# A two-block transformer on one core: GpSimd adds the shift rows behind w_out, VectorE squares the first feed-forward's relu

## The chip, the core and the metric

The kernel runs on one core of a Trainium2 chip. A core has TensorE (PE, the matrix engine), VectorE (DVE), ScalarE (ACT), GpSimd (POOL) and SyncE (SP, which here only issues DMAs); each engine works through its own queue in order and waits on semaphores. The metric is device time in microseconds (us), as the median of several runs. Lower is better.

## What is computed

Two transformer blocks on a sequence of 1024 rows of 1024 float32 values. What matters here of the first is its feed-forward, and of the second its output projection and the norm that follows:

```python
# first block, last step
h = h + jnp.square(jax.nn.relu(_rms_norm(h, norm_ff_g[l]) @ ff_w1[l])) @ ff_w2[l]
return _rms_norm(h, final_norm_g)
...
# second block
mod = c_act @ w_ada[l] + b_ada[l]
sh1, sc1, ga1, sh2, sc2, ga2 = [m[:, None, :] for m in jnp.split(mod, 6, axis=-1)]
...
x = x + ga1 * (mixed @ w_out[l])
h2 = rmsnorm(x, g_ffn[l]) * (1.0 + sc2) + sh2
gate, up = jnp.split(h2 @ w_gu[l], 2, axis=-1)
x = x + ga2 * ((jax.nn.silu(gate) * up) @ w_down[l])
```

The feed-forward is 1024 to 4096 to 1024 in the first block. `sh2` is one row of 1024 values that is added to every row.

## The kernel before, in words

The kernel is written as a row of phases. In each, every engine has its own program (`@block.tensor`, `@block.vector` and so on), all engines meet at the phase's end, and the order of the instructions on an engine is the order in which the program writes them. A float32 product is computed as three float32r matmuls on high and low halves (`mm3`, L187 to L189), so each left and right operand exists as a rounded high part (written by ScalarE) and a low part (VectorE: value minus high part). PSUM has 8 banks of 128 x 512 float32.

**The first feed-forward** (`phase_ffn` with `gated=None`, L2417) runs over 16 groups `g` of 256 hidden features. A group has an up half of four units `u = 4g + 2f + half` (two blocks `f` of 128 features, two halves of 512 rows) into banks 0 to 3, and a down half of 16 tiles (two column halves of 8 row tiles) into banks 4 to 7. TensorE runs up(g) and then down(g-1). For each unit ScalarE takes the relu out of PSUM into `first[half]` (L2556), GpSimd squares it into `full[half]` (L2600), ScalarE rounds it to the high part (`ft.hi`, L2543), and VectorE makes the low part (L2626). VectorE also adds the 16 down tiles to `h` (L2634, `sums`), makes the low parts of the next weights (L2620, L2667), and in the first 12 groups does eight multiply-adds for the second block's modulation, two behind each unit (`ModulationSum.add`, L2220 and L2223). TensorE writes down tile t+4 into the bank of tile t, so it waits for VectorE's sum of tile t. Signals: `bank_free` is raised by the relu, `square_done` by the square, `ft_hi` and `ft_lo` by the two parts.

VectorE's program in a group is: for each of the four units m, the low part of unit m-1, then two multiply-adds; behind the fourth also the low part of a down weight; then two sums, the low part of the fourth unit, two sums, a weight, and so on.

**The second block's output projection** (`phase_rows_gemm_norm` with `modulated`, L1810) multiplies by w_out in four sweeps p of eight row tiles t: column half c = p // 2, inner half p % 2. A row tile is 12 matmuls of 128x512. In the last sweep the norm runs beside the matmuls (`StreamNorm`, L281). Row t goes through: VectorE adds PSUM to the residual (L1933, `add`), ScalarE squares and sums (L308), takes a root (L350), VectorE inverts it (L355) and scales the row by it and the gain (L360) into one of two buffers `tmp[t % 2]`, TensorE turns the row (`turn`: 8 blocks of 128x128) into two banks, ScalarE writes the high part (L387, `high`), and VectorE the low part (L392, `low`). TensorE does turn(t-2) behind the matmuls of tile t. The shift `sh2` enters in the turn: the banks are begun with two matmuls of the shift row's high and low part (L371, L372, on 8 partitions), and then the row's blocks are multiplied by the identity and accumulated (L378) instead of transposed (L376). `ShiftRows` (L410) makes the two parts; they are loaded with a 4 KB DMA.

The orders that decide what waits for what in the last sweep:

```python
# VectorE, t = 0 .. 9
add(1, t); norm.scale(dve, t - 1); norm.low(dve, t - 2)
# ScalarE, t = 0 .. 9
norm.high(act, t - 2); norm.square(act, TT + t); norm.root(act, t)
```

The same phase runs twice in the first block without modulation: there `turn` is 8 transposes (L376) and nothing is added. GpSimd in this phase only scales two weight pieces by the gate (L1908).

Of the kernel before, what the change touches and what calls it, by code (L numbers as in the profile page):

```python
# [14 lines left out]
P = 128  # L15
# [105 lines left out]
class Core:  # L121


    def __init__(self, nc, ap):
# [10 lines left out]
            "bank_free", "ft_hi", "ft_lo", "table0", "table1", "table2", "table3", "mirrored", "selected", "row_ready_dve", "probs_turned", "mod_ready", "bias_zero", "ada_bias0", "ada_bias1", "mod_loaded", "mod_gain_loaded", "mod_summed", "mod_out", "mod_gain_ready", "mod_stored", "x_stored", "gate_loaded", "half_squared", "half_gained", "half_second", "row_base", "row_first", "row_bias", "shift_loaded", "shift_hi", "shift_lo", "row_squared", "row_root", "row_inverse", "row_scaled", "row_turned", "row_hi", "row_lo", "gain_loaded", "x0", "x1", "x2", "x3", "x4", "x5", "x6", "x7", "ada0", "ada1", "ada2", "ada3", "ada_summed", "ada_spilled", "w2_scaled", "mirror_copied",  # L135
# [145 lines left out]
class StreamNorm:  # L281
# [5 lines left out]
    def __init__(self, core, h, dst, gain, tmp_kb, junk_kb, ready, pairs=None, first_gain=None, shift=None):  # L287
        self.core, self.h, self.dst, self.gain, self.ready, self.pairs = core, h, dst, gain, ready, pairs
        self.first_gain, self.shift = first_gain, shift
# [72 lines left out]

    def turn(self, pe, t):
        nc, S = self.core.nc, self.core.sig
        pe.wait_ge(S["row_scaled"].sem, S["row_scaled"].at(t + 1))
# [28 lines left out]
    def close(self):  # L394
# [5 lines left out]
        if self.dst is not None:  # L400
            for n in ("row_turned", "row_hi", "row_lo"):
                S[n].close(TT)
        if self.first_gain is not None:
# [1406 lines left out]
def phase_rows_gemm_norm(core, lhs, w, h, dst, gain_name, gain_kb, tmp_kb, junk_kb, residual, ring_kb=(102, 118, 134), ahead=0, following=(), modulated=None):  # L1810
# [11 lines left out]
    summed = lambda n: S["dve_free"].at(n + 1)  # L1822
    shift, carried = None, core.tiny2[:, 256:264]
    if modulated is not None:
        gate, next_gate, shift = core.view(modulated[0], D), core.view(modulated[1], D), ShiftRows(core, modulated[2], 3 * D)
    norm = StreamNorm(core, h, dst, gain, tmp_kb, junk_kb, (S["dve_free"], summed), BEHIND, shift=shift and shift.operands())
    plain_gain = gain if modulated is None else norm.tmp[:, 0, :]
    with nc.Block() as block:
        @block.sync
        def _(sp):  # L1830
            for p in range(4):
# [6 lines left out]
                if p == R - 1:  # L1838
# [12 lines left out]
        def _(pe):  # L1851
            def turn(t):
# [5 lines left out]
                if t == 0 and modulated is not None:  # L1858
                    pe.wait_ge(S["shift_lo"].sem, S["shift_lo"].at(1))
                norm.turn(pe, t)  # L1860

            for p in range(4):
                c, kh = p // 2, p % 2
                pe.wait_ge(S["w_lo"].sem, S["w_lo"].at(p + 1))
                for t in range(TT):
# [8 lines left out]
                    if p == 3 and t >= 2:  # L1874
                        turn(t - 2)
# [1384 lines left out]
```

## Time and profile before

| | us |
|---|---|
| median of 3 runs | 4066.36 (4063.68 to 4066.87) |
| the profiled execution, its device time | 4063.24 |
| its span, first to last instruction | 4061.4 |
| TensorE busy | 3631.5 (89%) |
| VectorE busy | 1998.9 (49%) |
| ScalarE busy | 1121.2 (28%) |
| GpSimd busy | 541.7 (13%) |
| mean granted TensorE clock, 1 is full speed | 0.937 |

The first feed-forward fills about 1617 to 2340 us of the span, the last sweep of the second block's output projection with its norm 3259 to 3311 us. The percentages are averages over phases with different limits; what a change is worth has to be read in its own phase.

### The profile page before, as it was taken

The numbers are of one execution on the slowest core, as the hardware profiler recorded it, in microseconds if no ns is written. First come the engines' busy times: TensorE is split into PE (matmuls) and PEld (weight loads), VectorE is DVE, ScalarE is ACT, GpSimd is POOL, SyncE is SP. The second block draws the span as 40 slices with busy tenths as digits, with TensorE's granted clock in tenths as the row PEclk, the third lists the DMA queues.
The fourth block names the chain that finished last, engine by engine and source line by source line (L and its number), as shares of the span: only waits on it lengthen the run. The fifth ranks groups of instructions, "written<-read, shape, count | busy, mean of one in ns | idle before, by whom it ended". The sixth has DMA issues, their size and how long they took to land. (4 is left out here: it accounts for less than half of the span.)

```text
span 4061.4 us, 43012 instructions
## 1 busy us (share of the span) xinstructions
PE 3631.5 (89%) x16474; PEld 2856.8 (70%) x16474; DVE 1998.9 (49%) x3148; ACT 1121.2 (28%) x2006; POOL 541.7 (13%) x377
## 2 busy tenths in 40 slices
PE   7868696896978879999999998889989899999998
PEld 6736475773667757788888775766668777888886
DVE  3264645314744143555553438789975433333243
ACT  3233232323333132211211324124445321111112
POOL 0046564000010000101100100000034201000000
PEclk8969798897989999999999999999999999999999
DMA  2012123100022111323221211100000211111111
GB/s 94 27 33 74 42 79 106 31 32 4 1 91 83 57 47 34 97 93 121 93 93 60 84 52 37 47 20 22 11 14 1 99 37 52 52 49 49 47 52 52
DMA packets 210515, 220.07 MB, mean 54 GB/s; under 512 B 15523, under 2 KB 148548, under 8 KB 210098
## 3 DMA queue, kind: packets, MB, share of 16 engines
q1 hardware_dynamic: 210356, 217.90, 16.9%
q8 instruction: 106, 1.74, 0.2%
q14 instruction: 53, 0.43, 0.0%
HBM read 205.79 MB, written 11.55 MB: 54 GB/s over the span
## 5 line engine op out<-in xcount | busy, mean ns | idle before, releaser
L187 PE MATMUL psum<-rounded,rounded 128*128 128x512 f32 (+2 forms) x3936 | 1544.7, 392 | 216.5 <-POOL rounded L906 86.0
L188 PE MATMUL psum<-rounded,rounded 128*128 128x512 f32 (+2 forms) x3936 | 1536.2, 390 | 0.0
L189 PE MATMUL psum<-rounded,rounded 128*128 128x512 f32 (+2 forms) x3936 | 1534.1, 390 | 0.0
L187 PEld LDWEIGHTS psum<-rounded,rounded 128*128 128x128 f32 x3936 | 752.0, 191 | 384.0 <-POOL rounded L906 90.8
L189 PEld LDWEIGHTS psum<-rounded,rounded 128*128 128x128 f32 x3936 | 751.4, 191 | 153.1
L188 PEld LDWEIGHTS psum<-rounded,rounded 128*128 128x128 f32 x3936 | 751.9, 191 | 150.2 <-issue 0.2
L2634 DVE TENSOR_TENSOR plain<-psum,plain 128x512 f32<-128x512 f32 x432 | 288.5, 688 | 112.0 <-PE psum L189 110.6
L2645 DVE TENSOR_TENSOR plain<-psum,plain 128x512 f32<-128x512 f32 x44 | 30.4, 692 | 437.3 <-ACT plain L2554 437.3
L3052 POOL TENSOR_TENSOR plain<-plain,plain 128x128 f32<-128x128 f32 (+3 forms) x64 | 89.4, 1408 | 717.4 <-ACT plain L3123 695.4
L2626 DVE TENSOR_TENSOR rounded<-plain,rounded 128x512 fp32r<-128x512 f32 x108 | 97.2, 900 | 174.8 <-ACT rounded L2543 174.7
L2915 DVE MAX8 plain<-plain 128x8 f32<-128x384 f32 (+5 forms) x192 | 170.6, 889 | 4.0
L2917 DVE MATCH_REPLACE8 plain<-plain,plain 128x384 f32<-128x384 f32 (+5 forms) x192 | 168.1, 876 | 0.0
L2554 ACT ACTIVATE plain<-psum 128x512 f32<-128x512 f32 x44 | 26.3, 599 | 470.3 <-PE psum L189 470.3
L2612 POOL TENSOR_TENSOR plain<-plain,plain 128x1024 f32<-128x1024 f32 x22 | 53.4, 2429 | 748.2 <-DMA plain<-in_w_down_dram 748.2
L2990 PE MATMUL psum<-plain,plain 64*128 64x512 f32 (+7 forms) x384 | 151.2, 502 | 0.0
L906 POOL TENSOR_TENSOR rounded<-plain,rounded 128x512 fp32r<-128x512 f32 x96 | 133.3, 1402 | 128.9 <-ACT rounded L901 128.7
L2600 POOL TENSOR_TENSOR plain<-plain 128x512 f32<-128x512 f32 x64 | 67.2, 1050 | 606.2 <-ACT plain L2556 606.2
L2556 ACT ACTIVATE plain<-psum 128x512 f32<-128x512 f32 x64 | 38.3, 598 | 380.3 <-PE psum L189 380.3
L2576 ACT ACTIVATE rounded<-plain 128x1024 fp32r<-128x1024 f32 x54 | 57.1, 1057 | 278.6 <-DMA plain<-in_ff_w_dram 160.6
L3071 DVE CUSTOM_DVE_ANT_0 plain<-psum,plain 128x128 f32<-128x128 f32 (+7 forms) x128 | 96.4, 753 | 69.1 <-PE psum L2990 38.1
L3125 ACT ACTIVATE plain<-plain,plain 128x128 f32<-128x128 f32 (+7 forms) x128 | 98.8, 772 | 56.7 <-DVE plain L3074 56.0
L901 ACT ACTIVATE rounded<-plain 128x512 fp32r<-128x512 f32 x96 | 58.7, 629 | 178.3 <-DMA plain<-in_c_fwd_dram 103.5
(284 smaller groups left out, 3935.8 us busy)
## 6 DMA issues: line engine op xcount, KB each, us to landing
plain<-in_ff_w_dram SPq DMA_DIRECT2D x64, 512.0 KB, 5.5
plain<-in_w_ada_dram SPq DMA_DIRECT2D x96, 256.0 KB, 3.1
plain<-in_w_gu_dram SPq DMA_DIRECT2D x44, 512.0 KB, 4.9
plain<-in_w_in_dram SPq DMA_DIRECT2D x36, 512.0 KB, 3.7
plain<-in_c_fwd_dram SPq DMA_DIRECT2D x64, 256.0 KB, 2.6
plain<-in_w_down_dram SPq DMA_DIRECT2D x22, 512.0 KB, 3.2
plain<-in_c_inv_dram SPq DMA_DIRECT2D x32, 256.0 KB, 2.6
plain<-in_x_dram SPq DMA_DIRECT2D x2, 4096.0 KB, 15.5
```

Source lines behind the costliest of these rows:

```text
L187: nc.tensor.matmul(out, wh, xh, start=first, stop=False)
L188: nc.tensor.matmul(out, wh, xl, start=False, stop=False)
L189: return nc.tensor.matmul(out, wl, xh, start=False, stop=last)
L906: self.core.nc.gpsimd.tensor_tensor(w.lo, w.raw, w.hi_raw, ALU.subtract).then_inc(S["ft_lo"].sem, 1)
L2626: nc.vector.tensor_tensor(ft[b].lo[:, f, cols], full[half], ft[b].hi_raw[:, f, cols], ALU.subtract).then_inc(S["ft_lo"].sem, 1)
L2634: nc.vector.tensor_tensor(hv, ps[:, 4 + t % 4, :], hv, ALU.add).then_inc(S["dve_free"].sem, 1)
L2915: nc.vector.max(best, sc).then_inc(self.done, 1)
L2917: nc.vector.match_replace(out=sc, in_to_replace=best, in_values=sc, imm_value=TAKEN).then_inc(self.done, 1)
L2990: last = nc.tensor.matmul(ps[:, 2 * (n % 2) + a // BANK, 0:b - a], q, k[:, a:b], start=True, stop=True)
L3052: nc.gpsimd.tensor_tensor(tb[n % 2][:, 0:w], biases[h % 2][:, L - w:L], sel_tile(core, i), ALU.add).then_inc(S["pool_done"].sem, 1)
L3071: nc.vector.tensor_tensor_reduce(out=sc[n % 2][:, 0:w], in0=pair(n, w), in1=b, scale=SCALE, scalar=-3.0e38, op0=ALU.add, op1=ALU.max, accu ...
L3125: nc.scalar.activation(sc[n % 2][:, 0:w], sc[n % 2][:, 0:w], ACT.Exp, bias=stat[:, n % 16, 1:2], accum_out=stat[:, n % 16, 2:3]).then_inc( ...
```

## The change

It has two parts that share nothing.

In the first feed-forward, GpSimd no longer squares. VectorE multiplies the unit's PSUM bank by its relu (`first[half]`), which gives the same square. It does this at the head of each unit in its program, before the low part of the unit before. TensorE's bank is now free when the square is done.

Behind w_out the shift is a full tile of 1024 columns, the same row on all 128 partitions. It is loaded by a 512 KB DMA into the place of the first gate, once the fourth weight piece is scaled. GpSimd adds it to each scaled row in `tmp`; TensorE waits for this (`row_added`) and turns the row with 8 transposes. TensorE does turn(t-3) behind tile t, not turn(t-2), so that turn(4) comes behind tile 7 and turns 5, 6 and 7 follow it. `ShiftRows` is no longer used here.

```diff
@@ StreamNorm
+    def add(self, pool, t, row):
+        nc, S, tmp = self.core.nc, self.core.sig, self.tmp[:, t % 2, :]
+        pool.wait_ge(S["row_scaled"].sem, S["row_scaled"].at(t + 1))
+        nc.gpsimd.tensor_tensor(tmp, tmp, row, ALU.add).then_inc(S["row_added"].sem, 1)
+
     def turn(self, pe, t):
-        pe.wait_ge(S["row_scaled"].sem, S["row_scaled"].at(t + 1))
+        if self.added:
+            pe.wait_ge(S["row_added"].sem, S["row_added"].at(t + 1))
+        else:
+            pe.wait_ge(S["row_scaled"].sem, S["row_scaled"].at(t + 1))
@@ phase_rows_gemm_norm
+    late = 2 if modulated is None else 3
-        gate, next_gate, shift = core.view(modulated[0], D), core.view(modulated[1], D), ShiftRows(core, modulated[2], 3 * D)
-    norm = StreamNorm(core, h, dst, gain, tmp_kb, junk_kb, (S["dve_free"], summed), BEHIND, shift=shift and shift.operands())
+        gate, next_gate, shift = core.view(modulated[0], D), core.view(modulated[1], D), core.view(modulated[0], D)
+    norm = StreamNorm(core, h, dst, gain, tmp_kb, junk_kb, (S["dve_free"], summed), BEHIND, added=modulated is not None)
@@ its SyncE
-                        shift.load(sp)
+            if modulated is not None:
+                sp.wait_ge(S["w2_scaled"].sem, S["w2_scaled"].at(4))
+                sp.dma_start(shift, core.modulations[:, 3 * D:4 * D].partition_broadcast(P)).then_inc(S["shift_loaded"].sem, 16)
@@ its TensorE
-                if t == 0 and modulated is not None:
-                    pe.wait_ge(S["shift_lo"].sem, S["shift_lo"].at(1))
-                    if p == 3 and t >= 2:
-                        turn(t - 2)
-            turn(6)
-            turn(7)
+                    if p == 3 and t >= late:
+                        turn(t - late)
+            for t in range(TT - late, TT):
+                turn(t)
@@ its ScalarE, VectorE
-                shift.high(act)
-                    shift.low(dve)
@@ its GpSimd
+                pool.wait_ge(S["shift_loaded"].sem, S["shift_loaded"].at(16))
+                for t in range(TT):
+                    norm.add(pool, t, shift)
@@ phase_ffn, TensorE (gated is None)
-                            pe.wait_ge(S["bank_free"].sem, S["bank_free"].at(u - 3))
+                            pe.wait_ge(S["square_done"].sem, S["square_done"].at(u - 3))
@@ phase_ffn, GpSimd
-                            nc.gpsimd.tensor_tensor(full[half], first[half], first[half], ALU.mult).then_inc(S["square_done"].sem, 1)
-                over_groups(pool, squares)
@@ phase_ffn, VectorE
-                    if gated is not None:
-                        dve.wait_ge(S["act_done"].sem, S["act_done"].at(u + 1))
-                        if not (known(u) and u < 2):
-                            dve.wait_ge(S["ft_lo"].sem, S["ft_lo"].at(u - 1))
-                        nc.vector.tensor_tensor(full[half], ps[:, 2 * half + 1, :], first[half], ALU.mult).then_inc(S["square_done"].sem, 1)
+                    dve.wait_ge(S["act_done"].sem, S["act_done"].at(u + 1))
+                    if not (known(u) and u < 2):
+                        dve.wait_ge(S["ft_lo"].sem, S["ft_lo"].at(u - 1))
+                    bank = 2 * half + 1 if gated is not None else 2 * f + half
+                    nc.vector.tensor_tensor(full[half], ps[:, bank, :], first[half], ALU.mult).then_inc(S["square_done"].sem, 1)
```

VectorE in the first feed-forward's loop, from the low part of the third unit (before) or the square of the fourth (after) to the first sum of the group. L numbers of the changed kernel are some lines higher: L2626 is L2629, L2223 is L2235, L2667 is L2670, L2634 is L2637. Before:

```order
L2626 TENSOR_TENSOR rounded_2048_7326<-plain_512_1401,rounded_2048_7325 128x512 [waits ft_hi]
L2222 REGISTER_ALU [waits ada2]
L2223 SCALAR_TENSOR_TENSOR plain_512_10320<-plain_512_1409,plain_64_52,plain_512_10320 128x512 [waits ada_summed]
L2222 REGISTER_ALU [waits ada3]
L2223 SCALAR_TENSOR_TENSOR plain_512_10320<-plain_512_1408,plain_64_52,plain_512_10320 128x512 [waits ada_summed]
L2666 ISA
L2667 TENSOR_TENSOR rounded_1024_67<-plain_1024_70,rounded_1024_64 128x1024 [waits v_hi]
L2632 REGISTER_ALU
L2634 TENSOR_TENSOR plain_8192_4835<-psum,plain_8192_4835 128x512 [waits aux_done]
```

And in the changed kernel:

```order
L2648 TENSOR_TENSOR plain_512_1400<-psum,plain_512_1396 128x512 [waits ft_lo,act_done]
L2627 REGISTER_ALU
L2629 TENSOR_TENSOR rounded_2048_7326<-plain_512_1401,rounded_2048_7325 128x512 [waits ft_hi]
L2234 REGISTER_ALU [waits ada2]
L2235 SCALAR_TENSOR_TENSOR plain_512_10320<-plain_512_1409,plain_64_52,plain_512_10320 128x512 [waits ada_summed]
L2234 REGISTER_ALU [waits ada3]
L2235 SCALAR_TENSOR_TENSOR plain_512_10320<-plain_512_1408,plain_64_52,plain_512_10320 128x512 [waits ada_summed]
L2669 ISA
L2670 TENSOR_TENSOR rounded_1024_67<-plain_1024_70,rounded_1024_64 128x1024 [waits v_hi]
L2635 REGISTER_ALU
L2637 TENSOR_TENSOR plain_8192_4835<-psum,plain_8192_4835 128x512 [waits aux_done]
```

One instruction more, the square, stands ahead of an order that is otherwise the same.

TensorE in the last sweep of the second block's output projection, one turn and the matmuls behind it (`plain_896_49` holds the identity, `plain_2048_9062` the two row buffers, `rounded_8_...` the shift's parts). Before:

```order
L371 MATMUL psum<-rounded_8_21830,rounded_128_21828 128x512 [waits row_scaled,dve_free]
L372 MATMUL psum<-rounded_8_21830,rounded_128_21829 128x512
L378 MATMUL psum<-plain_896_49,plain_2048_9062 128x128 x4
L371 MATMUL psum<-rounded_8_21830,rounded_128_21828 128x512
L372 MATMUL psum<-rounded_8_21830,rounded_128_21829 128x512
L378 MATMUL psum<-plain_896_49,plain_2048_9062 128x128 x4
L187 MATMUL psum<-rounded_2048_9617,rounded_8192_21649 128x512
```

And in the changed kernel:

```order
L187 MATMUL psum<-rounded_2048_9617,rounded_8192_21622 128x512
L188 MATMUL psum<-rounded_2048_9618,rounded_8192_21622 128x512
L189 MATMUL psum<-rounded_2048_9617,rounded_8192_21623 128x512
L384 MATMUL psum<-plain_896_49,plain_2048_9062 128x128 [waits row_added,dve_free]
L384 MATMUL psum<-plain_896_49,plain_2048_9062 128x128 x7
L187 MATMUL psum<-rounded_2048_9617,rounded_8192_21622 128x512
```

The four matmuls of the shift are gone, the eight products with the identity are transposes (L384 is L376 of before), and the wait is on GpSimd's addition. GpSimd's queue in that phase, from the two scaled weight pieces on, before:

```order
L1908 TENSOR_TENSOR plain_2048_9057<-plain_2048_9057,plain_1024_19025 128x2048 [waits loaded2]
L1908 TENSOR_TENSOR plain_2048_9619<-plain_2048_9619,plain_1024_19025 128x2048 [waits loaded0]
L1828 UNCONDITIONAL_BRANCH
L2605 UNCONDITIONAL_BRANCH [waits barrier_Pool_Activation_PE_DVE_SP_gather]
L2612 TENSOR_TENSOR plain_1024_66<-plain_1024_66,plain_1024_21826 128x1024 [waits loaded]
```

And in the changed kernel:

```order
L1918 TENSOR_TENSOR plain_2048_9057<-plain_2048_9057,plain_1024_18998 128x2048 [waits loaded2]
L1918 TENSOR_TENSOR plain_2048_9619<-plain_2048_9619,plain_1024_18998 128x2048 [waits loaded0]
L366 TENSOR_TENSOR plain_2048_9062<-plain_2048_9062,plain_1024_18998 128x1024 [waits row_scaled,shift_loaded]
L366 TENSOR_TENSOR plain_2048_9062<-plain_2048_9062,plain_1024_18998 128x1024 [waits row_scaled] x7
L1839 UNCONDITIONAL_BRANCH
```

Eight additions of 128x1024 come behind the weight pieces, each waiting for VectorE's scaled row.

## Rows read from the trace of the kernel before

**Rows 1.** Waits, 1620 to 2345 us: engine, line, waited for: us in total, times, longest.

```profile
PE psum L187 <- DVE rounded L2620: 5.6, 1, 5.6
PE psum L187 <- DVE plain L2634: 2.0, 11, 0.2
```

**Rows 2.** Timeline, one group: start, us, engine, line, operation, shapes, count, [idle before].

```profile
1760.47 0.60 ACT L2556 ACTIVATE plain<-psum 128x512 f32<-128x512 f32 x1 [3.37 <-PE psum L189]
1761.22 1.04 POOL L2600 TENSOR_TENSOR plain<-plain 128x512 f32<-128x512 f32 x1 [4.40 <-ACT plain L2556]
1761.62 1.19 DVE L2626 TENSOR_TENSOR rounded<-plain,rounded 128x512 fp32r<-128x512 f32 x1 [2.79 <-ACT rounded L2543]
1764.18 1.22 DVE L2667 TENSOR_TENSOR rounded<-plain,rounded 128x1024 fp32r<-128x1024 f32 x1
1765.31 1.28 DVE L2634 TENSOR_TENSOR plain<-psum,plain 128x512 f32<-128x512 f32 x2
1765.48 0.39 PE L189 MATMUL psum<-rounded,rounded 128*128 128x512 f32 x1
1766.05 0.50 PE L187 MATMUL psum<-rounded,rounded 128*128 128x512 f32 x1 [0.18 <-DVE plain L2634]
1766.51 0.68 DVE L2626 TENSOR_TENSOR rounded<-plain,rounded 128x512 fp32r<-128x512 f32 x1
```

**Rows 3.** Stretches: length, PE, PEld, DVE, ACT, POOL busy, PEclk, DMA, GB/s.

```profile
3262.00:3308.00 46.00, 45.51 (x237) 33.87 (x236) 25.29 (x31) 14.64 (x31) 0.00 (x0) 1.00 0.14 37
1252.00:1262.00 10.00, 2.79 (x23) 2.13 (x20) 6.72 (x8) 5.55 (x10) 0.00 (x0) 0.93 0.06 16
20.00:25.00 5.00, 3.06 (x16) 2.43 (x16) 4.91 (x7) 3.42 (x8) 0.00 (x0) 0.66 0.76 184
```

**Rows 4.** Timeline, TensorE: two turns with the shift, two of the first block's w_out without.

```profile
3276.59 0.48 PE L187 MATMUL psum<-rounded,rounded 128*128 128x512 f32 x1
3282.77 0.48 PE L187 MATMUL psum<-rounded,rounded 128*128 128x512 f32 x1
...
1240.75 1.03 PE L376 MATMUL psum<-plain,plain 128*128 128x128 f32 x8
1244.36 1.04 PE L376 MATMUL psum<-plain,plain 128*128 128x128 f32 x8
1254.12 1.06 PE L376 MATMUL psum<-plain,plain 128*128 128x128 f32 x8 [1.46 <-DVE plain L360]
```

**Rows 5.** Timeline, VectorE, the last sweep: two additions, a scaled row, the last low part.

```profile
3261.88 0.75 DVE L1933 SCALAR_TENSOR_TENSOR plain<-plain,plain,psum 128x512 f32<-128x512 f32 x1 [22.84 <-PE psum L189]
3264.53 0.75 DVE L1933 SCALAR_TENSOR_TENSOR plain<-plain,plain,psum 128x512 f32<-128x512 f32 x1 [1.90 <-PE psum L189]
3265.39 1.28 DVE L360 SCALAR_TENSOR_TENSOR plain<-plain,plain,plain 128x1024 f32<-128x1024 f32 x1
3310.07 1.23 DVE L392 TENSOR_TENSOR rounded<-psum,rounded 128x1024 fp32r<-128x1024 f32 x1 [2.74 <-ACT rounded L387]
```

**Rows 6.** Groups by line and shape; one line's durations (min/median/max ns).

```profile
L387 ACT ACTIVATE rounded<-psum 128x1024 fp32r<-128x1024 f32 x32 | 32.8, 1025 | 64.5 <-PE psum L378 39.9 <-PE psum L376 24.5
L3052 POOL TENSOR_TENSOR plain<-plain,plain 128x1024 f32<-128x1024 f32 x8 | 18.9, 2357 | 3.4 <-DVE plain L3071 3.4
L1074 POOL TENSOR_TENSOR plain<-plain,plain x16: 1292/1742/1762, 346.6 to 614.5; 128x512 f32<-128x512 f32 x16
```

**Rows 7.** Timeline, VectorE beside a GpSimd instruction that reads SBUF.

```profile
3188.97 8.85 DVE L1916 TENSOR_TENSOR rounded<-plain,rounded 128x2048 fp32r<-128x2048 f32 x2 [3.22 <-ACT rounded L1889]
3190.66 5.01 POOL L1908 TENSOR_TENSOR plain<-plain,plain 128x2048 f32<-128x2048 f32 x1 [5.43 <-DMA plain<-in_w_out_dram]
3227.60 4.47 DVE L1916 TENSOR_TENSOR rounded<-plain,rounded 128x2048 fp32r<-128x2048 f32 x2
...
2322.05 10.76 POOL L314 TENSOR_TENSOR plain<-plain,plain 128x512 f32<-128x512 f32 x8 [33.31 <-ACT plain L308]
2323.17 0.69 DVE L2634 TENSOR_TENSOR plain<-psum,plain 128x512 f32<-128x512 f32 x1 [0.67 <-PE psum L189]
```

More of the change, by code:

```diff
@@ L281, with __init__ @@
 class StreamNorm:
-    def __init__(self, core, h, dst, gain, tmp_kb, junk_kb, ready, pairs=None, first_gain=None, shift=None):
+    def __init__(self, core, h, dst, gain, tmp_kb, junk_kb, ready, pairs=None, first_gain=None, shift=None, added=False):
         self.core, self.h, self.dst, self.gain, self.ready, self.pairs = core, h, dst, gain, ready, pairs
-        self.first_gain, self.shift = first_gain, shift
+        self.first_gain, self.shift, self.added = first_gain, shift, added
         self.tmp = core.view3(tmp_kb, 2, D)
@@ L402, in close @@
                 S[n].close(TT)
+        if self.added:
+            S["row_added"].close(TT)
         if self.first_gain is not None:
@@ L1889, in _ @@
                 nc.scalar.activation(ring[p % R].hi, ring[p % R].raw, ACT.Copy).then_inc(S["w_hi"].sem, 1)
-            if modulated is not None:
-                shift.high(act)
             for n in range(TT):
@@ L1961, in phase_rows_gemm_norm @@
     if modulated is not None:
-        shift.close()
+        S["shift_loaded"].close(16)
         S["w2_scaled"].close(4)
@@ L2525, in _ @@
             if modulation is not None:
-                pe.wait_ge(S["bank_free"].sem, S["bank_free"].at(4 * G))
+                pe.wait_ge(S["square_done"].sem, S["square_done"].at(4 * G))
                 tail.total(pe)
@@ L2555, in group @@
                         else:
-                            nc.scalar.activation(first[half], ps[:, 2 * f + half, :], ACT.Relu).then_inc(S["bank_free"].sem, 1)
+                            nc.scalar.activation(first[half], ps[:, 2 * f + half, :], ACT.Relu).then_inc(S["act_done"].sem, 1)
                         if (f, half) != (0, 0):
@@ L2592, in _ @@
             def _(pool):
-                def squares(g, b, n):
-                    for f in range(2):
-                        for half in range(2):
-                            u = unit(g, f, half)
-                            pool.wait_ge(S["bank_free"].sem, S["bank_free"].at(u + 1))
-                            if not (known(u) and u < 2):
-                                pool.wait_ge(S["ft_lo"].sem, S["ft_lo"].at(u - 1))
-                            nc.gpsimd.tensor_tensor(full[half], first[half], first[half], ALU.mult).then_inc(S["square_done"].sem, 1)
                 modulation.clear(pool)
-                over_groups(pool, squares)
                 tail.multiply(pool)
@@ L2639, in group @@
                     u = unit(g, f, half)
-                    if gated is not None:
-                        dve.wait_ge(S["act_done"].sem, S["act_done"].at(u + 1))
-                        if not (known(u) and u < 2):
-                            dve.wait_ge(S["ft_lo"].sem, S["ft_lo"].at(u - 1))
-                        nc.vector.tensor_tensor(full[half], ps[:, 2 * half + 1, :], first[half], ALU.mult).then_inc(S["square_done"].sem, 1)
+                    dve.wait_ge(S["act_done"].sem, S["act_done"].at(u + 1))
[3 more added lines that the diff above has]
+                    nc.vector.tensor_tensor(full[half], ps[:, bank, :], first[half], ALU.mult).then_inc(S["square_done"].sem, 1)
                     if m:
@@ L2684, in phase_ffn @@
         S[n].close(k * G)
-    if gated is None:
-        S["bank_free"].close(4 * G)
-    else:
-        S["act_done"].close(4 * G)
+    S["act_done"].close(4 * G)
+    if gated is not None:
         S["w2_scaled"].close(2 * G)
```

4 lines of the change are left out of this document (2 added, 2 removed).

## The prediction

> **What bounds the kernel now.** TensorE is busy 89% of the span, so a gain has to come from a pause or from work of TensorE itself. I read the two stages that the change touches, first by the waits, then by the timeline. "No change" is within 0.2%, 8.1 us, about what a measurement of this kernel can tell.
>
> In the first feed-forward TensorE hardly pauses: one wait of 5.6 us for VectorE's weight part (L2620) in the first group, and 11 short ones for a sum (L2634) [rows 1]. One of the 11 is drawn out [rows 2]: a matmul takes 0.23 us of TensorE (additions 2.65 to 2.7 us apart for tiles of 12 [rows 5]), but the one behind 1765.48 starts at 1766.05, so it is 0.34 late. It waits for the first sum of the group (1765.31), which VectorE began late. Looking back: ScalarE's relu ends at 1761.07, GpSimd squares 1761.22 to 1762.26, and VectorE's low part, begun at 1761.62, takes 1.19 us. The same instruction takes 0.68 at 1766.51, with no GpSimd work beside it.
>
> In the last sweep of the second block's output projection TensorE is the bound: 45.5 of 46 us busy at full clock [rows 3]. One tile with its turn takes 6.18 us (3276.59 to 3282.77); the same phase in the first block takes 3.61 (1240.75 to 1244.36) with plain transposes [rows 4]. So 2.57 us per row is the price of the shift on TensorE. From the first addition to the end of the last low part the sweep takes 3261.88 to 3311.30, 49.4 us [rows 5].
>
> **What GpSimd's port does.** Two low parts of 128x2048 take 4.47 us when GpSimd rests, and 8.85 when GpSimd scales a weight (5.01 us) meanwhile [rows 7]: the 4.4 us more say that VectorE stood still for most of GpSimd's instruction. But a sum out of PSUM takes 0.69 us in the middle of GpSimd's work [rows 7], no more than alone. I take from this: VectorE with two SBUF operands and GpSimd exclude each other; VectorE with one operand in PSUM is free. The Trainium skill says the same (SBUF — State Buffer, "Who interferes with whom"): the loser blocks for the whole instruction. By that rule the feed-forward's part of the change is helped and the sweep's part is hurt, since VectorE's scaled row reads h and the gain from SBUF.
>
> **Part 1, the square on VectorE.** GpSimd's 64 squares go. VectorE gets 64 instructions out of PSUM of the kind of L2634, 0.61 to 0.69 us each (two in 1.28), and three low parts of four lose the 0.51 us of blocking [rows 2]. At the critical place: relu ends 1761.07; square 1761.11 to 1761.72; low part 0.6, to 1762.3; the two multiply-adds with the low part of the down weight up to the first sum keep their distance of 2.6 us behind the low part (1761.62 + 1.19, less 0.08 by which neighbours overlap, is 1762.73; the sum starts at 1765.31); so the first sum starts at 1764.9 to 1765.0, not 1765.31. TensorE's 0.34 us of lateness is just covered: 11 x 0.34 = 3.8 us less. In the first group the same 0.3 us is taken from the one long wait, whose weight part stands behind the fourth unit. Sum 4.1 us less. The modulation's rows, for which VectorE waits early in a group, are asked for at TensorE's pace; the squares stand ahead of that wait only where their relu is done before the rows land, so I cost this at nothing. TensorE's wait for `square_done` of four units earlier looks back a whole group: nothing. Bounds: 0 (the pause stays, because something else is late) and 5.
>
> **Part 2, the addition on GpSimd.** Removed: the shift's four matmuls per row and the slower products; a 4 KB DMA and three tiny instructions ahead of the sweep, where TensorE does not wait for them. Added: a 512 KB DMA on SyncE's queue behind the fourth scaled weight, 30 us before it is needed and ahead of nothing that is due; and 8 GpSimd instructions of 128x1024. L3052 does such an addition in 2.36 us; L1074, the dearest per element, needs 1.74 for half the size, 3.5 for this [rows 6]. I take 2.36, since both its operands are plain rows as here.
>
> TensorE alone would go at 3.61 a row. The new bound is the chain of a row, because two row buffers and the orders on VectorE and ScalarE close a loop over two rows: low(t-2) stands ahead of add(t+1), and scale(t) needs it. From one scaled row to the next but one: scale 1.28, hand-over to GpSimd 0.15 (as relu to square in rows 2), addition 2.36, hand-over 0.1, turn 1.0 (1.06 when it stands alone [rows 4]), high part 1.03 [rows 6], hand-overs 0.15, low part 1.15 (1.23 less the overlap), and 0.9 from an addition's start to its scaled row (3264.53 to 3265.39 [rows 5]): 8.1 us for two rows, 4.05 each. The port alone would give scale 1.28, addition 2.36 and hand-overs, some 3.9: nearly the same.
>
> The sweep then, counted from the first addition: first scaled row done at 4.8 [rows 5], added at 7.3; TensorE's fourth tile ends at 3 x 2.7 = 8.1 (the pace of the additions in rows 5); turn(0), high, low until 11.3; add and scale of row 2 until 13.5; GpSimd until 16.0; turn(2) at 16.1. Five rows of 4.05 bring turn(7) to 36.35, and turn, high and low part end it at 39.6. Against 49.4 this is 9.8 less.
>
> The clock: behind tile 7, TensorE only turns four rows in some 13 us. In the first block, 28% busy with turns, it kept full clock for most of 1252 to 1262 us (mean 0.93) [rows 3]: it fell near 1260.6, 8.8 us behind the last matmul. So I expect the last turn at half speed, about 0.9 us more. Between 0 and two turns, 1.8.
>
> **Sum.** -4.1 - 9.8 + 0.9 = -13.0 us. Against the profiled execution's own 4063.24 us this is 4050.2. That execution is 3.1 us below the median of the runs shown, 4066.36; the same difference gives 4053.4 us.
>
> **The rivals.** (a) GpSimd's addition is dear: 3.5 us, or it also stops VectorE's instructions out of PSUM. The first makes a row 1.28 + 3.5 + 0.3 = 5.1 us or a little less in total, and the sweep 47; the second puts low part and addition behind GpSimd too, about 6 a row, and the sweep 49.5. For it: GpSimd instructions of up to 1.74 for 512 columns exist. Against it: rows 7 and the plain form. Then only part 1 and 0 to 2.6 us remain: 4061 to 4063.
>
> (b) Part 1 brings nothing: VectorE gets 0.2 to 0.7 us more work per unit, and if the low part stays at 1.19 us without GpSimd beside it, the first sum starts at 1765.5 and the pause remains. Against it stands the 0.68 of rows 2. 4066.4 - 8.9 = 4057.5.
>
> (c) Slower: TensorE's clock falls to half in the sweep. Now it has no pause there; then it has 0.4 us per row, and transposes where it had products. Tile and turn would take 5.1 + 1.9 = 7.0 us, more than the 6.18 of now. With eight tiles so, less the overlap at the start, and the last four turns at half speed behind them, I get 60.7 for the sweep, 11.3 more; less 4.1, and some 0.5 for the next phase's start: 4074. The total is slower from a row of 6.8 us on: 16.1 + 5 x 6.8 + 3.3 = 53.4, 4.0 more than now, which is what part 1 saves. For it: with transposes only, 60% busy, the clock fell to a mean of 0.66 in 20 to 25 us [rows 3]. Against it: the first block's same phase ran its sweep with these transposes at 3.61 a row, which is full clock [rows 4].
>
> The page TensorE: Matmul & The Clock Gate ("Part 4: PE-mode transpose") has it that transposes do not count as busy time for the clock; by that rule (c) and a slow end of the sweep become likelier, and the first block's rows speak against the first of these.
>
> (d) VectorE and GpSimd do not exclude each other here: the sweep saves 1 us more, within the range.
>
> **How the numbers follow.** Forecast, with (d): 0.73, own range 4048 to 4058. (a) 0.12, (b) 0.10, (c) 0.05. The range goes from 4046 (0.3% of scatter downward, the upper bounds of both gains) to 4063, to take in (b) and most of (a). Faster by over 0.2% (below 4058.2): the forecast but for a small part, and most of (b): 0.78. Within: (a), the rest of (b) and half of (c): 0.18. Slower: 0.04.
>
> **What would show it.** In the feed-forward the 11 waits for L2634's successor are gone, the low parts take 0.68, and the long wait is 5.3. In the sweep the additions of VectorE are 4.0 to 4.1 us apart, GpSimd's takes 2.36, TensorE waits for GpSimd, and from first addition to last low part it is 39 to 41 us. It is wrong if GpSimd's additions take over 3 us, if VectorE's low parts out of PSUM stretch beside them, if the sweep's clock is below 0.9, or if a new wait for a square appears on ScalarE or TensorE in the feed-forward.

## The result, and the profile after

| | before | after |
|---|---|---|
| median, us | 4066.36 (4063.07 to 4068.52, 15 runs) | 4073.59 (4069.27 to 4075.57, 15 runs) |
| profiled execution, device time | 4063.24 | 4071.82 |
| its span | 4061.4 | 4070.0 |
| mean granted TensorE clock | 0.937 | 0.93 |

The change makes the kernel slower: 1.0018 times the time before, 95% interval 1.0010 to 1.0025. The forecast was 4053.4 us, 20 less than measured, and 4073.59 lies outside its range.

Both parts did what they were to do. First the feed-forward: waits of the changed kernel, 1620 to 2345 us (engine, line, waited for: us in total, times, longest).

```profile
PEld psum L187 <- DVE rounded L2623: 5.7, 1, 5.7
PE psum L187 <- DVE rounded L2623: 5.3, 1, 5.3
PEld psum L187 <- DVE plain L2637: 2.1, 11, 0.2
PE psum L379 <- DVE plain L360: 0.7, 1, 0.7
```

The matmuls' row of 11 waits for a sum [rows 1] is gone. The weight loads (PEld), which run ahead of the matmuls, still wait at these 11 places, but shorter. Before, their row was

```profile
PEld psum L187 <- DVE plain L2634: 6.6, 11, 0.6
```

The long wait fell from 5.6 to 5.3. The timeline of the changed kernel in the same group as [rows 2], VectorE and the relu:

```profile
1759.71 0.60 ACT L2568 ACTIVATE plain<-psum 128x512 f32<-128x512 f32 x1 [3.37 <-PE psum L189]
1760.34 0.69 DVE L2648 TENSOR_TENSOR plain<-psum,plain 128x512 f32<-128x512 f32 x1 [2.70 <-ACT plain L2568]
1760.94 0.68 DVE L2629 TENSOR_TENSOR rounded<-plain,rounded 128x512 fp32r<-128x512 f32 x1
1761.54 1.53 DVE L2235 SCALAR_TENSOR_TENSOR plain<-plain,plain,plain 128x512 f32<-128x512 f32 x2
1762.99 1.22 DVE L2670 TENSOR_TENSOR rounded<-plain,rounded 128x1024 fp32r<-128x1024 f32 x1
1764.13 1.28 DVE L2637 TENSOR_TENSOR plain<-psum,plain 128x512 f32<-128x512 f32 x2
```

The low part takes 0.68 us, not 1.19, and the first sum starts 3.8 us behind the relu's end, 0.4 sooner than before (4.2). The last relu of the feed-forward is at 2282.47 us, 4.55 sooner than before (2287.02). Counted from the feed-forward's own first matmul, which comes 0.24 us later in this execution than in the one before, it is 4.8 us:

```profile
1618.14 0.79 PE L187 MATMUL psum<-rounded,rounded 128*128 128x512 f32 x1 [6.43 <-DVE rounded L2620]
1618.38 0.79 PE L187 MATMUL psum<-rounded,rounded 128*128 128x512 f32 x1 [6.43 <-DVE rounded L2623]
```

(the kernel before, then the changed one).

Then the sweep. VectorE and GpSimd in the changed kernel (L1945 is L1933 of before, L400 is L392); rows of other lines between them are left out:

```profile
3279.15 0.75 DVE L1945 SCALAR_TENSOR_TENSOR plain<-plain,plain,psum 128x512 f32<-128x512 f32 x1 [22.84 <-PE psum L189]
...
3284.09 2.39 POOL L366 TENSOR_TENSOR plain<-plain,plain 128x1024 f32<-128x1024 f32 x1 [41.71 <-DVE plain L360]
3285.38 2.19 DVE L360 SCALAR_TENSOR_TENSOR plain<-plain,plain,plain 128x1024 f32<-128x1024 f32 x1
3287.65 2.40 POOL L366 TENSOR_TENSOR plain<-plain,plain 128x1024 f32<-128x1024 f32 x1 [1.17 <-DVE plain L360]
3289.18 1.23 DVE L400 TENSOR_TENSOR rounded<-psum,rounded 128x1024 fp32r<-128x1024 f32 x1 [1.61 <-ACT rounded L395]
3290.32 0.74 DVE L1945 SCALAR_TENSOR_TENSOR plain<-plain,plain,psum 128x512 f32<-128x512 f32 x1
...
3306.57 0.74 DVE L1945 SCALAR_TENSOR_TENSOR plain<-plain,plain,psum 128x512 f32<-128x512 f32 x1
...
3318.18 1.23 DVE L400 TENSOR_TENSOR rounded<-psum,rounded 128x1024 fp32r<-128x1024 f32 x1 [2.57 <-ACT rounded L395]
```

From the first addition to the end of the last low part it is 40.3 us, against 49.4 [rows 5]. The sum of the two gains is 13.7 us, and the kernel is 8.6 longer in its span. So I went through the trace between the two places, comparing when the same instructions come. The gap turns over in one spot: `BlockTail`, the norm behind the first feed-forward, where TensorE turns the finished rows (`turns`, with the shift matmuls, 16 half rows). Its stretch before and after (length, PE, PEld, DVE, ACT, POOL busy, mean granted clock, DMA, GB/s), first of the kernel before:

```profile
2341.50:2369.10 27.60, 27.48 (x160) 20.16 (x160) 21.39 (x28) 12.97 (x29) 5.77 (x4) 1.00 0.21 86
```

and of the changed kernel:

```profile
2337.00:2385.40 48.40, 48.39 (x160) 35.08 (x160) 21.33 (x28) 13.12 (x28) 5.71 (x4) 0.53 0.12 49
```

The same 160 instructions of TensorE, dense in both, take 27.5 us at clock 1.00 (2.4 GHz) and 48.4 us at 0.53, which is the level of 1.2 GHz (0.50) but for the start. That is 20.9 us, in code that the change does not touch. The timeline of TensorE there, in the kernel before:

```profile
2341.56 0.45 PE L371 MATMUL psum<-rounded,rounded 8*128 8x512 f32 x1 [0.75 <-DVE plain L360]
2342.16 1.16 PE L378 MATMUL psum<-plain,plain 128*128 128x128 f32 x8
2343.88 1.16 PE L378 MATMUL psum<-plain,plain 128*128 128x128 f32 x8
2345.59 1.16 PE L378 MATMUL psum<-plain,plain 128*128 128x128 f32 x8
```

and in the changed one:

```profile
2337.01 0.45 PE L379 MATMUL psum<-rounded,rounded 8*128 8x512 f32 x1 [0.75 <-DVE plain L360]
2337.61 1.16 PE L386 MATMUL psum<-plain,plain 128*128 128x128 f32 x8
2339.32 1.94 PE L386 MATMUL psum<-plain,plain 128*128 128x128 f32 x8
2342.34 2.08 PE L386 MATMUL psum<-plain,plain 128*128 128x128 f32 x8
```

In both TensorE comes from matmuls without a pause at full clock, waits 0.75 us for the first scaled row, and starts to turn. In one it keeps 2.4 GHz, in the other it falls within 3 us of the first turn and stays at 1.2 until the turns end.

The gap between the traces (after less before) is thus: -4.5 us up to the turns; +15.1 at the phase behind them and the next one's first matmuls (L2851 of before, at 2434.9 and 2450.0), which is -4.5, +20.9 and 1.2 given back where the next matmuls take 56.4 us and not 57.6; +17.2 at the start of the second block's output projection, so some 2 us more on the way, whose places I did not follow; -9.2 in the sweep, so +8.1 at its end; and +8.6 at the end of the span, where the last half us was not followed either.

### The profile page after: what moved, and what is told of

Its sections match the earlier page's. It is cut to its first block and busy times, and to the rows that moved or that the text cites. A ratio compares the mean times of both kernels' runs of the same rounds, so it can differ in the third digit from the quotient of the medians.

```text
span 4070.0 us, 42805 instructions
## 1 busy us (share of the span) xinstructions
PE 3636.3 (89%) x16378; PEld 2863.8 (70%) x16378; DVE 2015.7 (50%) x3211; ACT 1121.0 (28%) x2004; POOL 492.7 (12%) x321
## 5 line engine op out<-in xcount | busy, mean ns | idle before, releaser
L2648 DVE TENSOR_TENSOR plain<-psum,plain 128x512 f32<-128x512 f32 x108 | 74.7, 692 | 657.0 <-ACT plain L2566 439.0
L2637 DVE TENSOR_TENSOR plain<-psum,plain 128x512 f32<-128x512 f32 x432 | 289.0, 688 | 111.8 <-PE psum L189 110.4
L314 POOL TENSOR_TENSOR plain<-plain,plain 128x512 f32<-128x512 f32 x16 | 22.5, 1411 | 706.7 <-ACT plain L308 706.3
L196 PE MATMUL psum<-plain 128*128 128x512 f32 x140 | 82.5, 679 | 19.6 <-PEq L2962 13.3
```

Of the source, the lines that this page charges most:

```text
L196: core.nc.tensor.matmul(core.psum[:, bank, :], core.ident, core.small[:, 0:4, :], start=True, stop=True)
L2637: nc.vector.tensor_tensor(hv, ps[:, 4 + t % 4, :], hv, ALU.add).then_inc(S["dve_free"].sem, 1)
```

## The experiments

A ratio below is the time over that of the kernel before, measured beside it, with its 95% interval. Theory T: both parts gain what was forecast, and the clock in `BlockTail`'s turns costs more than that. Theory R: the loss is in one of the parts. "Idle matmul" below is `keep_clock(core, n)`, n products of 128x512 with the identity whose result nobody reads; one shows as two records of L196 and takes 0.95 us at full clock.

### Each part alone

`ffn_part` has only the feed-forward's part of the diff, `sweep_part` only that behind w_out.

> Only the feed-forward's part: VectorE squares, the sweep behind w_out is that of before. Theory T (the time lost is TensorE's clock in the turns behind the first feed-forward, which fell because the 4.5 us gained there move those turns in time): the feed-forward ends 4.5 us sooner, the 16 halves of turns take 48 us instead of 27.5 (clock 0.5), the total is about 4066.4 - 4.5 + 20 = 4081 to 4082. Rival R (the loss comes from GpSimd's work or the longer load in the second part): 4062.

> Only the sweep's part: GpSimd adds the shift behind w_out, the feed-forward is that of before. T: the turns behind the first feed-forward stay at full clock (27.5 us), the sweep from its first addition to its last low part takes 40.3 instead of 49.4, the next phase starts at half clock for a little longer: 4066.4 - 8 = about 4058. R: slower than before, 4075 or more.

Measured: `ffn_part` 4084.46 us (4082.63 to 4086.38), ratio 1.0047 (1.0030 to 1.0064). `sweep_part` 4057.08 us (4055.06 to 4059.87), ratio 0.9980 (0.9970 to 0.9989), beside 4066.34 of the kernel before. The stretch of the turns in `ffn_part`:

```profile
2340.20:2388.70 48.50, 48.46 (x160) 35.16 (x160) 21.36 (x28) 13.14 (x28) 5.75 (x4) 0.53 0.12 49
```

Part 2 gains 9.3 us (forecast 8.9). Part 1 alone costs 18.1 (I had expected 15 to 16), and its trace has the same fall in the same turns. Theory R is out.

### Keep the clock, or move the turns, in the changed kernel

`hold` puts an idle matmul in the 0.75 us wait; `shift1` puts it into TensorE's work ahead of the modulation's column sums, so that the wait and the turns are the same and come 0.95 us later.

```diff
@@ hold: BlockTail.turns
+        keep_clock(self.core, 1, bank=0)
         for t in range(TT):
@@ shift1: BlockTail.total
         pe.wait_ge(S["mod_loaded"].sem, S["mod_loaded"].at(32))
+        keep_clock(self.core, 1, bank=0)
         for n in range(12):
```

> The changed kernel with one idle 128x512 product more on TensorE (0.9 us, its result is not used) ahead of the modulation's column sums, so everything behind the first feed-forward comes 0.9 us later. T: the turns are back at the place relative to the clock's earlier steps where they kept full clock, so the total falls by 19 to 20 us and the 0.9 is paid: 4054 to 4056. R (the change itself lowers the clock, wherever the turns lie): 4074 to 4075.

> The changed kernel with the same idle product put into the 0.75 us pause between the last down tile and the first turn behind the first feed-forward. If the pause is what lets the clock fall: the turns keep full clock, 4054 to 4055. If only the place in time counts: the pause is gone but the turns lie 0.2 us later, the clock falls as before, 4073 to 4074. R: 4073 to 4074 as well.

Measured: `shift1` 4052.42 us (4049.83 to 4056.85), ratio 0.9967 (0.9956 to 0.9979); `hold` 4054.66 (4052.86 to 4058.69), ratio 0.9973 (0.9962 to 0.9983). In `hold` the idle matmul fills the wait, and the turns begin without one:

```profile
2339.26 1.02 PE L196 MATMUL psum<-plain 128*128 128x512 f32 x2
2340.21 0.48 PE L379 MATMUL psum<-rounded,rounded 8*128 8x512 f32 x1
```

The stretch of the turns in `hold`:

```profile
2340.20:2367.80 27.60, 27.52 (x161) 20.16 (x160) 21.28 (x28) 12.88 (x29) 5.65 (x4) 1.00 0.21 85
```

and in `shift1`, whose wait of 0.75 us is still there:

```profile
2343.95 0.45 PE L379 MATMUL psum<-rounded,rounded 8*128 8x512 f32 x1 [0.75 <-DVE plain L360]
2343.90:2371.50 27.60, 27.48 (x160) 20.17 (x160) 21.37 (x28) 12.95 (x29) 5.75 (x4) 1.00 0.21 85
```

Either way the whole change is 12 to 14 us faster than the kernel before, as forecast (13.0); `shift1` came out below its expected range. The turns themselves, and the pause, are not enough to make the clock fall. Closing the pause is enough to prevent it: all 8 executions of `hold` lie between 4052.9 and 4058.7 us.

### Is it the change, or only the place in time?

Theory P: the fall needs the pause, but whether it comes is settled by where the turns lie in time. Rival Q: it needs the new feed-forward. Rival S: what helped was an idle matmul near the turns. `before_shift3` and `shift3` have three idle matmuls at the place of `shift1`, in the kernel before and in the changed one. `ffn_hold` is `ffn_part` with the line of `hold`.

> The kernel before, with three idle matmuls of 128x512 (2.8 us at full clock) ahead of the modulation's column sums. The down matmuls and the turns behind them end 2.8 us later, nothing else is altered. Theory P (what decides whether the clock falls in the turns is only where they come in time): either 4069, with turns of 27.5 us, or, where they come badly, 4088 to 4091 with turns of 48 us in the kernel that has none of the change. Rival Q (the fall needs the change itself: its feed-forward without the 11 short pauses): 4069 and turns of 27.5 us.

> The changed kernel with three idle matmuls where shift1 had one, 2.8 us in place of 0.9. Theory P (place in time alone): it need not go as shift1 did; 4056 with turns of 27.5 us, or 4076 with 48. Rival S (any idle matmul there is enough to hold the clock, wherever the turns come): 4054 to 4056, turns of 27.5 us.

> Part 1 alone (as ffn_part, 4084.5 and turns of 48.5 us), and one idle matmul in TensorE's 0.75 us wait ahead of the first turn. If the fall starts from that wait: turns of 27.5 us and 4062 to 4064, which is 4066.4 less part 1's 4.1, and 0 to 1.5 us more. If the idle matmul only helped in hold by moving things by 0.2 us: 4083 to 4085 as ffn_part.

Measured: `before_shift3` 4067.50 us (4063.10 to 4071.24), ratio 0.9999 (0.9990 to 1.0009); `shift3` 4056.18 (4053.37 to 4058.26), ratio 0.9974 (0.9962 to 0.9985); `ffn_hold` 4061.40 (4057.68 to 4064.03), ratio 0.9984 (0.9974 to 0.9994), beside 4066.28 of the kernel before. All three have turns of 27.5 us at clock 1.00. `ffn_hold` confirms `hold` (10 executions of 10) and gives part 1 its price: 4.9 us less. The first two tell P from Q and S in nothing, since P allowed both outcomes. So three variants more were tried, one of them in the kernel before, and one whose turns are moved from far off:

```diff
@@ before_place: BlockTail.total of the kernel before
+        keep_clock(self.core, 2, bank=0)
+        for _ in range(3):
+            self.core.nc.tensor.matmul(self.core.psum[:, 0, 0:P], self.core.ident, self.core.ident, start=True, stop=True)
@@ after_place: the same in the changed kernel, with 3 and 5
@@ early1: phase_ffn of the changed kernel, TensorE, group
                 up(g, b)
+                if modulation is not None and known(g) and g == 1:
+                    keep_clock(core, 1, bank=4)
```

> The kernel before, its turns put later by another amount: two idle matmuls of 128x512 and three of 128x128 ahead of the modulation's column sums, 2.3 us, where before_shift3 had 2.8 us and 4067.5. Theory P (place in time alone, to a fraction of a us): this is the place where the turns of the unchanged kernel should come as badly as those of the changed one; turns of 48 us and 4086 to 4090. Rival Q (the fall needs the change itself): turns of 27.5 us and 4067 to 4069.

> The changed kernel, its turns later by 3.4 us (three idle matmuls of 128x512 and five of 128x128), where shift1 had 0.9 and shift3 2.8 us and both kept the clock. Theory P: the place is bad again, turns of 48 us and 4076 to 4078. Rival S (an idle matmul ahead of the column sums holds the clock wherever the turns come): turns of 27.5 us and 4055 to 4057.

> The changed kernel with one idle matmul (0.9 us) 650 us ahead of the turns, between up(1) and down(0) of the feed-forward, and nothing near them. Theory P: it moves the turns by 0.9 us as shift1 does; turns of 27.5 us and 4052 to 4056. Rival S (the idle matmul has to stand near the turns to matter): turns of 48 us and 4074 to 4075.

Measured, beside 4066.47 us of the kernel before: `before_place` 4090.48 us as the median, ratio 1.0042 (1.0025 to 1.0059). Its ten executions fall apart in two kinds, 3 at 4066.0 to 4068.7 and 7 at 4087.6 to 4092.9, and neither number describes either kind. `after_place` 4057.74, ratio 0.9983 (0.9973 to 0.9992), also of two kinds: 8 at 4053.6 to 4058.8 and 2 at 4075.7 and 4077.4. `early1` 4052.62 (4050.66 to 4056.01), ratio 0.9969 (0.9957 to 0.9981). The turns in the profiled execution of `before_place`:

```profile
2349.60:2398.20 48.60, 48.55 (x160) 35.16 (x160) 21.31 (x28) 13.09 (x29) 5.68 (x4) 0.52 0.12 48
```

and its TensorE at their start:

```profile
2349.58 0.45 PE L371 MATMUL psum<-rounded,rounded 8*128 8x512 f32 x1 [0.75 <-DVE plain L360]
2350.18 1.16 PE L378 MATMUL psum<-plain,plain 128*128 128x128 f32 x8
2351.93 2.08 PE L378 MATMUL psum<-plain,plain 128*128 128x128 f32 x8
```

In the kernel before, which has none of the change, the clock falls in 7 executions of 10 when the turns come 2.2 us later, and in none when they come 2.5 us later. Q falls. S falls too: `early1` holds the clock with its idle matmul 665 us away, and `after_place` can lose it with idle matmuls close by. P has a miss as well: it expected the fall in `after_place`, and 8 of 10 executions kept the clock.

The place has to be counted from something within the program. From the start of the span it sorts nothing: the turns of `before_place` start at 2349.58 us and lose the clock, those of `before_shift3` start at 2349.51 and keep it. The 14 profiled executions reach the first feed-forward's first matmul at 1617.9 to 1624.4 us, earlier or later by chance. From that matmul to the turns they differ by what was changed or inserted, and by little else (`ffn_part` and the changed kernel by 0.03 us). All places together, by how much later the turns start behind it than in the kernel before (723.4 us), as the traces have it:

| turns later by, us | kernel | wait of 0.75 us | clock in the turns |
|---|---|---|---|
| -4.8 | after, `ffn_part` | there | falls (15 of 15 executions; 4 of 4) |
| -4.7 and -5.0 | `hold`, `ffn_hold` | filled | holds |
| -4.1 and -3.9 | `early1`, `shift1` | there | holds |
| -2.2 | `shift3` | there | holds |
| -1.1 | `after_place` | there | falls in 2 of 10 |
| 0 | before | there | holds |
| 2.2 | `before_place` | there | falls in 7 of 10 |
| 2.5 | `before_shift3` | there | holds |

The kinds are read from the times: where a kernel has both, they lie 16.9 us or more apart with nothing between, and the profiled executions agree. The two profiled executions of the divided kernels are both of the kind that falls.

The traces also have a reason why one kernel can give the same outcome every time. The clock's last step ahead of the turns is a rise early in the feed-forward, from 0.50 to 1.00. Two stretches on either side of it in the kernel before, and two in the changed one (columns as above):

```profile
1648.00:1653.20 5.20, 5.20 (x13) 4.04 (x14) 3.47 (x4) 0.00 (x0) 0.00 (x0) 0.50 0.79 261
1653.20:2369.00 715.80, 713.06 (x3149) 580.11 (x3147) 382.84 (x497) 163.60 (x271) 85.52 (x76) 1.00 0.27 90
1648.00:1653.40 5.40, 5.40 (x13) 4.18 (x14) 1.94 (x2) 0.00 (x0) 0.00 (x0) 0.50 0.54 188
1653.40:2339.00 685.60, 684.85 (x2999) 561.19 (x2998) 380.66 (x535) 152.61 (x251) 18.75 (x14) 1.00 0.28 92
```

This rise comes 34.9 to 35.1 us behind the feed-forward's first matmul in all 14 profiled executions, whatever the kernel and whenever the span began. So program and clock steps already stand in step there. Programs that are alike up to the turns then have the same distance from that rise to the turns: 683.6 us in the changed kernel and 683.7 in `ffn_part`, which both lose the clock, and 688.4 in the kernel before and in `sweep_part`, which both keep it. In `shift1` it is 684.6. That no execution of one program lies elsewhere is inferred from these pairs; each program was profiled once.

### The sweep's end

`drain` is `hold` with two idle matmuls in each of TensorE's waits ahead of turns 5, 6 and 7.

```diff
@@ phase_rows_gemm_norm, TensorE, turn
+                if modulated is not None and t >= 5:
+                    keep_clock(core, 2, bank=2 * BEHIND[t])
                 norm.turn(pe, t)
```

> hold (4054.7) with two idle matmuls (1.9 us at full clock) in TensorE's waits for GpSimd's addition ahead of turns 5, 6 and 7 of the sweep (each waits 1.9 to 2.6 us). If the three slow turns (1.94 us each, not 1.05) are the clock's: they take 1.05, the chain behind tile 7 is 2.7 us shorter, and the next phase starts at full clock: 4050 to 4052. If the clock has fallen already before the first of these waits: the idle matmuls take 3.7 us at half clock and put each turn later by 1 us or more: 4056 to 4059.

Measured: 4052.11 us (4049.39 to 4054.21), ratio 0.9964 (0.9950 to 0.9978), so 2.5 less than `hold`. Turns 5, 6 and 7 of `hold`, of which two are slow in the profiled execution:

```profile
3289.76 1.07 PE L384 MATMUL psum<-plain,plain 128*128 128x128 f32 x8 [2.52 <-POOL plain L366]
3294.25 1.94 PE L384 MATMUL psum<-plain,plain 128*128 128x128 f32 x8 [3.42 <-POOL plain L366]
3297.75 1.94 PE L384 MATMUL psum<-plain,plain 128*128 128x128 f32 x8 [1.56 <-POOL plain L366]
```

and of `drain`:

```profile
3285.84 1.09 PE L384 MATMUL psum<-plain,plain 128*128 128x128 f32 x8 [0.75 <-POOL plain L366]
3290.29 1.09 PE L384 MATMUL psum<-plain,plain 128*128 128x128 f32 x8 [1.64 <-POOL plain L366]
3293.80 1.09 PE L384 MATMUL psum<-plain,plain 128*128 128x128 f32 x8 [0.70 <-POOL plain L366]
```

The turns take 1.09 us, so it was the clock. But their starts are no closer: 4.49 and 3.50 us apart in `hold`, 4.45 and 3.51 in `drain`. The chain over VectorE and GpSimd sets them, and a slow turn costs its 0.85 us only once, at the last. My expectation of 2.7 us counted it at every turn. Some 1 us more comes from the next phase, whose first 20 us run at a mean clock of 0.90 in `drain` and 0.85 in `hold`. That is 1.9 of the 2.5 us; the rest is within the scatter of either run.

`best` is `drain` with three idle matmuls at the start of two phases, ahead of TensorE's first wait.

```diff
@@ phase_cols_gemm (the call behind the turns) and phase_ffn (the second), TensorE, ahead of the first wait for w_lo
+                keep_clock(core, 3)
```

> drain (4052.1) with three idle matmuls (2.8 us) more at the start of two phases whose TensorE waits for the first weight's low part: the one behind the turns (idle 4.99 us, then some 6.8 us at half clock) and the second feed-forward (idle 6.12 us, then some 4 us at half clock). If the clock holds: 2 to 3 us less at each, 4046 to 4049. If it falls anyway, since half of each wait stays idle: 4052, or 1 to 2 more where the idle matmuls run at half clock into the first product.

Measured: 4052.05 us (4050.02 to 4054.33), ratio 0.9965 (0.9951 to 0.9978): the same as `drain`. Its TensorE at the start of the second feed-forward:

```profile
3303.12 4.51 PE L196 MATMUL psum<-plain 128*128 128x512 f32 x6 [2.64 <-PEq L1839]
3307.02 0.84 PE L187 MATMUL psum<-rounded,rounded 128*128 128x512 f32 x1
```

The 2.64 us between the phases cannot be filled from inside the next one, and the idle matmuls themselves then run partly at half clock: 4.5 us in place of 2.8. The first product starts 6.5 us behind the end of the last turn (3300.5), not 6.1 as in `drain`, but the 20 us from it on run at full clock (1.00, where `drain` has 0.90). Twelve products on, counted from the end of the last turn, that is some 1 us gained. At the other phase, behind `BlockTail`'s turns, it is 0.2: the first product starts 6.4 us behind the turns' end (5.0 in `hold`), and the half clock avoided is worth little more than this delay. The medians show no gain, and with five executions each, spread over 4 to 5 us, they cannot tell 1 us from none.

## Why the prediction was wrong

**Part 1, -4.1 us: right, 0.7 too little.** Measured -4.8 from the feed-forward's first matmul to the turns, and -4.9 in `ffn_hold`. The steps held one by one: the square takes 0.69, the low part 0.68, the 11 pauses go, the long wait loses 0.3, and no wait for a square appears on TensorE. ScalarE's 16 waits for one get shorter, 3.8 us in total against 10.9. The sum is slightly off in itself: 11 x 0.34 is 3.7, not 3.8. Rival (b) is out.

**Part 2, -9.8 us: right, 0.6 too much.** GpSimd's addition takes 2.34 to 2.42 us (forecast 2.36). The additions of VectorE come 3.6 and 4.5 us apart by turns, from 3290.32 to 3306.57 in four steps, 4.06 each (forecast 4.05): the loop over two rows was seen rightly, not its halves. The whole is 40.3 us, where 39.6 was forecast. The exclusion is in the rows above: the scaled row at 3285.38 takes 2.19 us beside a GpSimd addition where 1.28 is its time alone, the low part out of PSUM at 3289.18 takes its 1.23 beside another. That is what the Trainium skill says (SBUF — State Buffer, "Who interferes with whom"), and rivals (a) and (d) are out.

**The clock behind tile 7, +0.9 us: about right in size, for the wrong count.** Timeline of TensorE in the changed kernel, its last four turns:

```profile
3303.27 1.06 PE L384 MATMUL psum<-plain,plain 128*128 128x128 f32 x8 [0.65 <-POOL plain L366]
3306.86 1.94 PE L384 MATMUL psum<-plain,plain 128*128 128x128 f32 x8 [2.53 <-POOL plain L366]
3311.34 1.94 PE L384 MATMUL psum<-plain,plain 128*128 128x128 f32 x8 [2.55 <-POOL plain L366]
3315.14 1.94 PE L384 MATMUL psum<-plain,plain 128*128 128x128 f32 x8 [1.86 <-POOL plain L366]
```

Three turns are slow, not one. The last costs 0.85 us. Turn 7 also comes 3.80 us behind turn 6, and 3.50 in `hold`, where turn 6 is slow as well but turn 5 is not; so turn 5 may cost another 0.3 us through the loop over two rows, which no run isolates.

**Rival (c): a fall of the clock, in the wrong place.** The total did become slower, and (c) even names 4074 us, half a us from what was measured. That is luck: its 11.3 us were to be lost in the sweep, and the sweep gained 9.2. The clock fell elsewhere, in turns that are no transposes. In the sweep the tiles ran at a mean of 0.99, and only the drain behind them at half, which brings the sweep's mean to 0.83; a sweep below 0.9 was named as a sign of being wrong, and it came without the loss that it was to announce:

```profile
3279.00:3306.00 27.00, 23.99 (x125) 19.49 (x123) 19.39 (x24) 11.39 (x25) 13.63 (x6) 0.99 0.26 66
3306.00:3316.00 10.00, 4.74 (x20) 4.02 (x21) 6.47 (x8) 3.25 (x7) 5.41 (x3) 0.50 0.00 0
```

**The step that failed is the sum**: "-4.1 - 9.8 + 0.9 = -13.0 us", with "I read the two stages that the change touches" ahead of it. It took the time of every other stage as fixed when they start some 4 us sooner, and gave no reason. The turns behind the feed-forward were not fixed: they need 27.5 us or 48.4, by their place in time, and that term, +20.9, was missing. With it the sum is +7.9 us, and 4074.3; measured 4073.6. `hold` and `shift1`, where the term is zero, give -11.7 and -13.9.

Could it have been foreseen? That this stage was open to it, yes. The pause of 0.75 us ahead of dense turns stands in the trace of before, and a stage of 27.5 us that would take some 20 more at half clock should have been a rival with a price. Which way it would go, no: in the kernel before the clock holds there, and the table above gives no more than that one step of 0.7 to 0.9 us decides. Of the seven places of the table with the pause open one falls always and two sometimes, and these two were picked from the traces' clock records as likely ones. My judgement is that a chance of one in five for it would have been honest.

That the changed kernel loses the clock in 15 executions of 15 fits the traces: by the clock's rise in the feed-forward, programs with the same code lie alike to the clock's steps. The Trainium skill has it (TensorE: Matmul & The Clock Gate, Part 1) that the monitor behind the clock runs freely and does not begin anew with a kernel; the traces do not contradict this, but they show the two in step by the time of the first feed-forward. What stays open is what brings them into step, and why at two places the executions are divided: of the divided kernels only executions that fell were profiled. Nor does any run show what in the pause and the turns makes one place hold and another fall.

## What to carry to other kernels

A change that only makes a stage end sooner moves everything behind it, and a dense stretch of TensorE that starts behind a short pause can come out at half clock for its whole length. So compare the two traces stage by stage by the granted clock before a gain or loss is put down to the edit; if the clock differs in code that was not touched, fill the pause with an idle matmul and measure the edit again. Here one such line turns the change from 7 us slower to 12 us faster, and it held in both kernels in which it was tried. Moving the stretch by inserted work helped too, but nothing keeps it there when the next edit moves it again. And count places from a matmul that both kernels share: from the start of the span two executions of one program differ by several us.

## What was not expected of the hardware

- The clock fell behind a pause of only 0.75 us, while TensorE was busy before and behind it, and stayed at 1.2 GHz for some 46 us of turns in which TensorE had no pause (48.39 of 48.40 us busy). These turns are products with the identity and the shift matmuls, no transposes. In the wait-free sweep of [rows 3] a mixture of the same turns and of 128x512 matmuls kept full clock.
- The Trainium skill (TensorE: Matmul & The Clock Gate, "Part 4: PE-mode transpose") has it that transposes do not count as busy time; here the stretch that stayed slow had none, so that rule does not cover it.
- GpSimd's addition of 128x1024 blocks VectorE's scaled row for 0.9 us (2.19 against 1.28), and VectorE's instructions out of PSUM not at all; here "GpSimd for SBUF, VectorE for PSUM" was a division of work that cost little.
